# First two projection tiles over each arriving chunk, last eight tiles by token thirds, in a hybrid decoder step

## What is computed

```python
xn = rmsnorm(h, p['norm_mix_a'][i])          # start of layer 0
proj = (xn @ w_in).astype(f32)
...
hid = jax.nn.relu(xn @ w_up)                 # end of layer 1
h = h + (hid * hid) @ w_down
...
y = rmsnorm(h, final_gain)                   # final norm, then the output
```

## Time and profile before

| | us |
|---|---|
| median of 3 runs (2941.95 to 2946.55) | 2943.44 |
| the profiled execution: time | 2947.95 |
| its span | 2946.2 |
| TensorE (PE) busy | 2837.9 |
| VectorE (DVE) busy | 1648.9 |
| ScalarE (ACT) busy | 354.7 |
| GpSimd (POOL) busy | 23.2 |

### The profile page before, as it was taken

The page is one execution under the profiler, slowest core; times in us unless marked ns, Lnnn a source line. Parts: engine busy times, 40 slices in busy tenths (PEclk is TensorE's granted clock), DMA queues, the critical chain, the costliest instruction groups (busy, mean ns, idle before and its releaser), DMA issues.

```text
span 2946.2 us, 42340 instructions
## 1 busy us (share of the span) xinstructions
PE 2837.9 (96%) x17818; PEld 2723.0 (92%) x17818; DVE 1648.9 (56%) x3052; ACT 354.7 (12%) x598; POOL 23.2 (1%) x25
## 2 busy tenths in 40 slices
PE   7998989999999999999999999999999999999997
PEld 6878878799889999999999999998899999999997
DVE  6657667566667536354366535456576355363554
ACT  4202213021221000000001111112130000000001
POOL 3000000000000000000000000000000000000000
PEclk9999999999999999999999999999999999999999
DMA  3100001021121111111112112022111111111111
GB/s 112 41 16 29 31 21 37 14 82 52 52 104 44 43 51 44 51 44 51 44 51 90 58 47 60 29 60 67 65 67 44 51 43 51 44 51 43 51 44 72
DMA packets 42685, 150.99 MB, mean 51 GB/s; under 512 B 5768, under 2 KB 7688, under 8 KB 41488
## 3 DMA queue, kind: packets, MB, share of 16 engines
q1 hardware_dynamic: 30528, 111.20, 11.9%
q10 hardware_dynamic: 11984, 37.22, 3.4%
HBM read 130.32 MB, written 18.08 MB: 50 GB/s over the span
## 4 chain that ended last, share of the span: by engine, by line
PE 75%; DVE 5%; issue 1%; ACT 1%; DMA 0%; ACTq 0%; DVEq 0%; SPq 0%
PE proj L336 66%; PE bank L391 7%; PE bank L378 1%; PE bank L388 1%; DVE x_lo L784 0%; PE bank L597 0%; DVE w_lo L700 0%; DVE s L739 0%; DVE w_hi L698 0%; DVE h L1374 0%; DVE s L900 0%; DVE s L899 0%; DVE s L898 0%; DMA w_raw<-w_all 0%; DMA s<-retention 0%
## 5 line engine op out<-in xcount | busy, mean ns | idle before, releaser
L336 PE MATMUL proj<-x_hi,w_hi 128*128 128x344 f32 x4788 | 1577.3, 329 | 21.9 <-DVE x_lo L784 8.3
L336 PE MATMUL proj<-x_lo,w_hi 128*128 128x344 f32 x4788 | 1542.5, 322 | 0.0
L336 PE MATMUL proj<-x_hi,w_lo 128*128 128x344 f32 x4788 | 1542.3, 322 | 0.0
L336 PEld LDWEIGHTS proj<-x_hi,w_hi 128*128 128x128 f32 x4788 | 912.5, 191 | 50.2 <-issue 37.8
L336 PEld LDWEIGHTS proj<-x_lo,w_hi 128*128 128x128 f32 x4788 | 913.0, 191 | 2.8 <-issue 0.9
L336 PEld LDWEIGHTS proj<-x_hi,w_lo 128*128 128x128 f32 x4788 | 912.2, 191 | 0.0
L1232 DVE TENSOR_TENSOR h<-h,proj 128x344 f32<-128x344 f32 x144 | 73.9, 513 | 372.2 <-PE proj L336 372.2
L700 DVE TENSOR_TENSOR w_lo<-w_raw,w_hi 128x1024 fp32r<-128x1024 f32 x202 | 247.5, 1225 | 7.0
L1217 DVE TENSOR_TENSOR mlp_t<-proj,rbc 128x344 f32<-128x344 f32 x192 | 99.0, 516 | 237.6 <-PE proj L336 223.9
L391 PE MATMUL bank<-s,s 128*128 128x128 f32 x1408 | 193.9, 283 | 9.2 <-DVE s L959 8.4
L391 PEld LDWEIGHTS bank<-s,s 128*128 128x128 f32 x1408 | 173.8, 195 | 14.9 <-DVE s L959 10.0
(11 more groups left out here) (266 smaller groups left out, 1754.0 us busy)
## 6 DMA issues: line engine op xcount, KB each, us to landing
w_raw<-w_all SPq DMA_DIRECT2D x204, 512.0 KB, 3.4
h<-x SPq DMA_DIRECT2D x8, 516.0 KB, 9.3
h<-x ACTq DMA_DIRECT2D x8, 516.0 KB, 6.5
h_spill<-h ACTq DMA_DIRECT2D x8, 516.0 KB, 2.7
h<-h_spill ACTq DMA_DIRECT2D x8, 516.0 KB, 6.4
y<-h ACTq DMA_DIRECT2D x8, 516.0 KB
sample_C<-state_c ACTq DMA_DIRECT2D x4, 1024.0 KB, 4.9
s_state_c<-sample_C ACTq DMA_DIRECT2D x4, 1024.0 KB
```

The costliest lines, as they stand in the source:

```text
L336: last = nc.tensor.matmul(PJ[:, tt, 0:TT], w[slot][:, k, :], x[:, k, tt * TT:(tt + 1) * TT], start=(at == 0 and j == 0), stop=(at == len(o ...
```

## The change

At the start both tile 0 and tile 1 are multiplied with each input chunk as it comes, tile 0 into banks 0 to 2 of MB, tile 1 into `proj`. ScalarE makes all three thirds of x_hi and one full-width square, VectorE adds the squares, and GpSimd has no work left. Tile 0's weights are split into a place of their own (`first_w`) before the wait for the constants. The three norm products stand among the last products of these tiles, and VectorE drains tile 1 before tile 0.

At the end the last eight down tiles run third by third: all eight tiles for third 0, then for third 1, then for third 2. So eight split tiles are kept (`last_w` holds six of them, where the operand of the up tiles was). The final norm, the gains and the stores go by thirds too: third tt-1 is normalised, scaled and stored while third tt is multiplied. The stores are 24 pieces of 128 x 344 and go through SP's queue.

The diff, cut:

```diff
+        first_w = (place("first_hi", [P, KC, P], F32R, at=region[1] + 14 * R),
+                   place("first_lo", [P, KC, P], F32R, at=region[1] + 15 * R))
+        last_w = [(place(f"last_hi{j}", ...), place(f"last_lo{j}", ...)) for j in range(6)]
...
@@ sync
-                if c == 2:
+                if c == 0:
                     sp.dma_start(raw[1][:], io["w_all"][1]).then_inc(w_loaded[1], 16)
...
+            for tt in range(NT):
+                for c in range(KC):
+                    sp.wait_ge(y_done, KC * tt + c + 1)
+                    sp.dma_start(io["y"][c][:, tt * TT:(tt + 1) * TT], H[:, c, tt * TT:(tt + 1) * TT]).then_inc(y_stored, 16)
+            sp.wait_ge(y_stored, 16 * KC * NT)
@@ gpsimd
-            for c in range(1, KC):
-                for tt in range(NT):
-                    pool.wait_ge(sq_made, 3 * c + tt + 1)
-                    ...
-                    nc.gpsimd.tensor_tensor(third(SSQ, tt), third(SSQ, tt), third(SQT, tt), ALU.add).then_inc(ssq_added, 1)
@@ tensor
+            def first_tiles(X):
+                hi, lo = X
+                pe.sem_inc(proj_full, 3)
+                for k in range(KC):
+                    for t in range(2):
+                        pe.wait_ge(w_split, t + 1)
+                        whi, wlo = first_w if t == 0 else (w_hi[w_slot(t)], w_lo[w_slot(t)])
+                        for tt in range(NT):
+                            pe.wait_ge(x_ready, 3 * k + tt + 1)
+                            if t == k == 0:
+                                claim(tt, "dve")
+                            out = PJ[:, tt, 0:TT] if t else MB[tt][:, 0:TT]
+                            for j, (w, x) in enumerate(((whi, hi), (whi, lo), (wlo, hi))):
+                                last = nc.tensor.matmul(out, w[:, k, :], x[:, k, tt * TT:(tt + 1) * TT], ...)
+                            ...
+                        if k == KC - 1:
+                            if t == 0:
+                                pe.wait_ge(ssq_first, 1)
+                            for tt in ((0, 1), (2,))[t]:
+                                b = (3, 4, 3)[tt]
+                                claim(b, "act")
+                                publish(nc.tensor.matmul(MB[b][:, 0:TT], ones, third(SSQ, tt), start=True, stop=True), b)
...
+            def last_down(t0, Y, ready):
+                hi, lo = Y
+                for tt in range(NT):
+                    for c in range(KC):
+                        t, turn = t0 + c, KC * tt + c
+                        whi, wlo = last_w[c - 2] if c >= 2 else (w_hi[w_slot(t)], w_lo[w_slot(t)])
+                        pe.wait_ge(w_split, t + 1)
+                        pe.wait_ge(proj_drained, 3 * t0 + turn - 2)
+                        for k in range(KC):
+                            if c == 0:
+                                pe.wait_ge(x_ready, ready + 3 * k + tt + 1)
+                            ...
+                        last.then_inc(proj_full, 1)
+                        if tt and c == 0:
+                            norm_third(tt - 1)
+                norm_third(NT - 1)
...
-            first_tile(XA)
-            norm_finish(0)
-            for _ in projections(T_AB, 4, XA):
+            first_tiles(XA)
+            for _ in projections(T_AB + 1, 3, XA):
                 pass
...
-            norm_finish(4)
@@ vector
+            def last_down(t0):
+                def gained(tt, c):
+                    if c == 0:
+                        v.wait_ge(*n.awaited(rbc_ready))
+                    hh = H[:, c, tt * TT:(tt + 1) * TT]
+                    stt(hh, hh, vcol(V_GAIN["final"] + c), third(rbc, tt), ALU.mult, ALU.mult).then_inc(y_done, 1)
+                for tt in range(NT):
+                    for c in range(KC):
+                        turn = KC * tt + c
+                        if tt == 0 and c < KC - 2:
+                            split(t0 + c + 2, 0, last_w[c])
+                        hh = H[:, c, tt * TT:(tt + 1) * TT]
+                        v.wait_ge(proj_full, 3 * t0 + turn + 1)
+                        tt_(hh, hh, PJ[:, turn % NT, 0:TT], ALU.add).then_inc(proj_drained, 1)
+                        v.wait_ge(*n.awaited(sq_made))
+                        if c:
+                            ...
+                            tt_(third(SSQ, tt), third(SSQ, tt), third(SQT, tt), ALU.add).then_inc(ssq_added, 1)
+                        if tt and 2 <= c < 6:
+                            gained(tt - 1, 2 * c - 4)
+                            gained(tt - 1, 2 * c - 3)
+                for c in range(KC):
+                    gained(NT - 1, c)
...
+            v.sem_inc(proj_drained, NT)
+            split(0, to=first_w)
             v.wait_ge(consts_in, 32)
...
-            split(0)
             for c in range(KC):
-                v.wait_ge(h_in[c], 16)
                 for tt in range(NT):
-                    if tt < HI_BY_ACT:
-                        v.wait_ge(*made)
-                    else:
-                        step(ts_(hi, hh, gain, None, ALU.mult))
-                    stt(lo, hh, gain, hi.bitcast(F32), ALU.mult, ALU.subtract).then_inc(x_ready, 1)
-            split(1)
+                    v.wait_ge(x_hi_made, 3 * c + tt + 1)
+                    stt(lo, H[:, c, tt * TT:(tt + 1) * TT], gain, hi.bitcast(F32), ALU.mult, ALU.subtract).then_inc(x_ready, 1)
+                if c == 0:
+                    split(1)
+                v.wait_ge(*n.awaited(sq_made))
+                if c == KC - 1:
+                    tt_(SSQ[:], SSQ[:], s[c][:], ALU.add).then_inc(ssq_first, 1)
+                elif c:
+                    step(tt_(SSQ[:], SSQ[:], s[c][:], ALU.add))
+            split(2)
...
-            refill(0)
-            first = projections(s, T_AB, 0, 4)
+            first = projections(s, T_AB, 0, 4)
             for tt in range(NT):
+                v.wait_ge(*n.awaited(rbc_ready))
+                next(first)
+            for tt in range(NT):
+                ps = take(tt)
+                ...
@@ scalar
+            a.dma_start(vec[:], io["vec"]).then_inc(consts_in, 16)
             a.dma_start(consts[:], io["consts"]).then_inc(consts_in, 16)
-            a.dma_start(vec[:], io["vec"]).then_inc(consts_in, 16)
...
             for c in range(KC):
                 a.wait_ge(h_in[c], 16)
                 for tt in range(NT):
-                    if tt < HI_BY_ACT:
-                        act(XH..., H..., ACT.Copy, scale=...)
-                    squares(c, c, tt, 0)
+                    act(XH..., H..., ACT.Copy, scale=...).then_inc(x_hi_made, 1)
+                act((s[c] if c else SSQ)[:], H[:, c, :], ACT.Square).then_inc(sq_made, 1)
...
+            for tt in range(NT):
+                for c in range(KC):
+                    a.wait_ge(proj_drained, 3 * t0 + KC * tt + c + 1)
+                    ...
+                    act(third(SQT if c else SSQ, tt), H[:, c, tt * TT:(tt + 1) * TT], ACT.Square).then_inc(sq_made, 1)
+                ps, r = take(tt), third(rbc, tt)
+                act(r, ps[:, 0:TT], ACT.Ln, bias=eps[:, 0:1], scale=1.0 / D_MODEL).then_inc(*done(tt))
+                act(r, r, ACT.Exp, scale=-0.5).then_inc(*n.made(rbc_ready))
```

More of the change, by code:

```diff
@@ L342, in tile_steps @@
                         yield
-            def first_tile(X):
+            def first_tiles(X):
                 hi, lo = X
-                pe.wait_ge(w_split, 1)
+                pe.sem_inc(proj_full, 3)
                 for k in range(KC):
[L349 to L354, removed]
-                        if k == KC - 1:
-                            last.then_inc(proj_full, 1)
+                    for t in range(2):
[7 more added lines that the diff above has]
+                            for j, (w, x) in enumerate(((whi, hi), (whi, lo), (wlo, hi))):
+                                last = nc.tensor.matmul(out, w[:, k, :], x[:, k, tt * TT:(tt + 1) * TT],
+                                                        start=(k == 0 and j == 0), stop=(k == KC - 1 and j == 2))
+                            if k == KC - 1 and t:
+                                last.then_inc(proj_full, 1)
+                            elif k == KC - 1:
+                                publish(last, tt)
+                        if k == KC - 1:
+                            if t == 0:
[4 more added lines that the diff above has]
+                                publish(nc.tensor.matmul(MB[b][:, 0:TT], ones, third(SSQ, tt), start=True, stop=True), b)
             def norm_finish(number):
-                pe.wait_ge(ssq_added, 21 * (number + 1))
+                pe.wait_ge(ssq_added, 21 * number)
                 for tt in range(NT):
@@ L611, in mlp, with norm_third @@
                         t = t0 + 16 * g + 8 + k
-                        tile(t, w_slot(t), Y, hid + 24 * g if k == 0 else None)
+                        if t0 == T_MLP0 or g < GROUPS - 1:
+                            tile(t, w_slot(t), Y, hid + 24 * g if k == 0 else None)
+                if t0 == T_MLP1:
```

(32 more changed lines are left out.)

44 lines of the change are left out of this document (19 added, 25 removed).

## The result

The changed kernel took 2916.12 us (median, 2914.77 to 2917.02), the kernel before 2943.26 us (2941.95 to 2946.55): 27.1 us less, ratio 0.9907 with a 95% interval of 0.9895 to 0.9919. Forecast were 2916.7 us and -26.7 us. Its profiled execution took 2914.77 us with a span of 2913.0 us.

A forecast was written before the change was run, and what follows sets the result against it. TensorE was taken as the bound, busy 2837.9 us of a 2946.2 us span. Terms -21.3 + 1.3 + 0.3 + 1.3 - 8.3 gave -26.7 us, from 2943.44 to 2916.7 us, range 2912 to 2925.

The forecast's parts named there:

- (a): Start, setup: tile 0's weight split moves ahead of the constants; TensorE's first product at 8.9 instead of 10.14.
- (b): Start, input pace: ScalarE 2.5 us and VectorE 2.75 us a chunk; last x_lo at 29.7, last sum at 31.
- (c): Start, TensorE: no longer short of data, product spacing falls at 15.5 (14 or 17), 144 products end at 34.6.
- Rival (1): First tiles: clock stays low throughout, tile 2 starts at 52.4, -12.1 us in all, 2931.3 us; chance 0.04.
- (e): Gates after the start: TensorE waits for a late drain of tile 2's second third, +1.3 us (0 to 2.5).
- (f): Last eight tiles, first third: only the second tile's weight split is late, +0.3 us (0 to 1.5).
- (g): Last tiles: two of three norm thirds now lie in the product stream, 0.63 us each, +1.3 us.
- (h): Tail behind the last product: 10.9 us in place of 19.15, -8.3 us (-9.3 to -7.2).
- (2): Start: x_lo stays at 1.1 us because ScalarE or TensorE slows VectorE; near 2930 us; chance 0.04.
- (3): Last eight tiles, first third: late splits and gaps drop TensorE to slow spacing; up to +17 us, 2961 us; chance 0.03.

The follow-up runs named there:

- second profile: Both kernels, unchanged, profiled once more, one execution each; spans 2942.3 us (kernel before) and 2914.0 us (changed kernel).
- drain_first: Changed kernel with VectorE draining tile 2's second third before it waits for ScalarE's part of the gate chain; 2914.41 us, ratio 0.9901.
- start_alone: Changed kernel with the end of the kernel before put back, so only the start is changed; 2924.25 us, ratio 0.9930.
- end_alone: Kernel before with only the end of the change: last down tiles and norm by thirds, stores on SP's queue; 2935.42 us, ratio 0.9974.
- ahead: As drain_first, and ScalarE starts the input chunks once the gains are in, without waiting for the other constants; 2913.53 us, ratio 0.9897.
- feed-alone kernel: Changed kernel with the new feed but only tile 0 over the arriving chunks, tile 1 following as a whole; 2922.57 us.

## Why the prediction was right

Its steps one by one, from the first pair of profiles.

- **(a) and (b), setup and feed.** First product 8.83 (8.9 forecast), last x_lo 29.4 (29.7), last sum 30.5 (31).
- **(c), the clock.** W, the time at which the spacing falls, was 13.46, not 15.5, and 12.07 in the second profile: below my lower end of 14. I had counted the 5.1 us of the earlier trace rows as the shortest run-up. The two executions had 15 and 10 slow products. Tile 2 began at 35.27 and 34.63 (36.5), a gain of 22.5 us instead of 21.3 in the first pair. Rival (1) did not come.
- **(e), the gate chain.** 1.0 us (1.3). The order of the waits was right, down to the next drain being just in time, as drain_first showed.
- **(f), late weights.** 0.2 us (0.3) for the second tile. VectorE's turn was 3.36 us, not 3.6. The tightest other split is that of the fourth tile, which waits 1.47 us for its weights:

```profile
2818.47 0.69 DVE L738 CAST last_hi<-w_raw 128x1024 fp32r<-128x1024 f32 x1 [1.47 <-DMA w_raw<-w_all]
...
2819.20 1.23 DVE L740 TENSOR_TENSOR last_lo<-w_raw,last_hi 128x1024 fp32r<-128x1024 f32 x1
...
2821.84 0.69 DVE L738 CAST last_hi<-w_raw 128x1024 fp32r<-128x1024 f32 x1
```

  It ends at 2820.43, and TensorE wants it at 2814.77 + 2 x 3.78 = 2822.3: 1.9 us of slack (2.1).
- **(g)** Two norm thirds of 0.58 us: 1.2 us (1.3).
- **(h), the tail.** 10.1 us against 10.9. The oversized term is the last store, 2.7 + 0.4 us forecast: its pieces landed 1.9 us after issue (median), also under the estimated 2.4 us that stands beside that sum, and the span ended 2.5 us after the last gain. Gain 9.0 instead of 8.3.

These sum to -22.5 + 1.0 + 0.2 + 1.2 - 9.0 = -29.1 us, 2.4 us more than forecast and 2.0 us more than the times show. A term is missing in the prediction, the stretch between: "behind tile 4 the mixers are as before" put it at nothing, and it isn't constant. In the two spans at hand it made the difference larger (-4.0 us without the wait, and -29.1 - 4.0 gives the 33.2 of the spans but for rounding), in the second pair smaller (+1.5: 2776.1 against 2774.6). That the medians came within 0.6 us of 2916.7 rests in part on such errors having cancelled: the ends were undersized by 2.4 us and the middle took back 2.0. Luck has a part in that. Whether the middle is longer on average behind the new start, or these are draws from one spread, stays open. For the first: start_alone missed its gain by 3.3 us in the same direction, and an estimate, each kernel's median time less its two ends in the traces and the 1.8 us around the span, leaves 2773.7 us for the kernel before and 2774.1 for end_alone, but 2777.1 for the changed kernel and 2777.5 for start_alone, each of these two with the 1.0 us of waiting. Without that wait, drain_first has 2775.3 and ahead 2774.3. For the second: two unchanged profiles of the kernel before differ by 3.8.

Of the rivals, (2) and (3) are answered by runs above: without GpSimd x_lo is fast, with it slow; and late splits cost their waits and not the clock.

## What to carry to other kernels

An engine off the critical path can set the pace through another one: 21 GpSimd additions, 23 us or 1% of the span, slow VectorE's feed from 2.7 to 4.7 us a chunk in the changed kernel, and leaving them out brought 8.3 us there, pairing the tiles 6.5. When an order is changed so that a resource is wanted three times as often, follow it turn by turn with its real slack; here 3.4 us of load and 3.4 us of VectorE's work a turn fitted 3.78 us because two buffers overlapped them. And where a kernel's middle varies by 2 to 4 us between executions, the difference of two spans proves nothing finer; compare the marks at both ends of what was changed.

## What the runs showed of the hardware that was not expected

TensorE's spacing did not follow its busy share at the start. In the feed-alone kernel, then in the kernel before:

```profile
12.20:30.60 18.40, 11.58 (x63) 9.78 (x63) 18.19 (x28) 15.70 (x26) 0.00 (x0) 1.00 0.38 151
```

```profile
16.50:33.00 16.50, 13.72 (x36) 9.44 (x36) 16.39 (x16) 11.63 (x23) 16.50 (x16) 1.00 0.06 26
```

The first ran at 0.16 us spacing, the 2.4 GHz level, with TensorE busy 11.58 of 18.40 us; the second at 0.29 us, the 1.2 GHz level, with 13.72 of 16.50 us. The view prints 1.00 for both, so it can't be used at the start. In the second profile of the kernel before the fast spacing appeared from 30.2 to 32.2 and was lost again. What lets it rise at 12.1 in one execution of the changed kernel and at 13.5 in another isn't settled by these runs, nor is what keeps it down from 10 to 34 in the kernel before. A store of 172 KB landed 1.9 us after its issue, less than the 2.7 us of the one of 162 KB in the earlier trace rows.
